# A hybrid encoder layer: SiLU of the next tile's streams and of z moved from the end of a slot to its middle

## Chip, cores and metric

One core of a Trainium2 chip runs the whole kernel. The metric is the device time of one execution in microseconds (us), the median of several runs.

## What is computed

One layer is applied to a prompt of 2048 positions and to a small batch of 8 x 16 positions. The prompt takes nearly all of the time. Cut to what matters here:

```python
p = rms_norm(x, norm1) @ w_in                    # 3080 columns: u_a v_a q k v z beta a
u_a, v_a = gelu(u_a), gelu(v_a)                  # group A: gMLP in blocks of 128 positions
y_a = rms_norm(u_a * (W_s @ v_a + b_s))
q, k, v = silu(causal_conv(q, k, v))             # group B: gated DeltaNet, 4 heads of 128
o, S = delta_rule(l2norm(q), l2norm(k), v, beta, g)   # needs the inverse of a triangular matrix
y_b = rms_norm(o, gdn_norm) * silu(z)
x = x + concat(y_a, y_b) @ w_o
x = x + (silu(h2 @ w_gate) * (h2 @ w_up)) @ w_down    # h2 = rms_norm(x, norm2)
```

## The kernel before

The kernel has two phases, one after the other. The first (`prompt_phase`) computes the token mixing of the prompt, the second (`out_phase`) the feed-forward part. The change touches the first phase alone.

The first phase works on 16 tiles of 128 positions. Two jobs are interleaved by hand on every engine. The background job is the dense work: items of 24 matmuls (three for each of 8 slices of the contraction, because fp32 values are split in a high and a low part), each item cut in four quarters of 6 matmuls. The items are the columns of w_in for 4 tiles at once and, in the last four slots, the product with w_o. The foreground job is the mixing of one tile t. A slot is 25 quarters long and holds the mixing of one tile; slot numbers run from -4 to 15, and `upto(t, n)` issues the background's quarters until n of slot t are out. The order of the instructions of every engine is fixed by this; the engines meet at semaphores only.

The background's steps on ScalarE (ACT) are `split_weights` (L675, the high part of the weights, at a quarter's part 1), `keep_item` (L695, L698 and L701, a copy of a finished item out of PSUM, at part 2) and `split_h` (L687). VectorE (DVE) makes the low parts (L1015, L1021), the taps of the convolution (L1030 to L1047) and, in the last slots, additions (L1077, L1081). TensorE (PE) waits at the start of item n for the low part of its weights, and for item n-2 to have been copied or added, since two PSUM banks take turns. L1535 to L1537 are the three matmuls.

The foreground on ACT, in a slot t: key norms (L891 to L898), values (L905), then six levels of the inverse. In level l PE makes a product (`level_lx`, L1850), ACT copies it (L915), PE makes the next (`level_xlx`, L1864, and L1870 for the last levels), DVE subtracts (L1403) and turns (L1406), and PE's next level starts. Two quarters lie in each level. Behind them come delta (L927), the output (L934), the decays of tile t+1 (L880, L883) and the output's norm (L873, L875). DVE multiplies with the norm (L1455) and with silu(z) (L1459), and TensorE turns v_a of the next tile (L1792). At the end of the slot ACT loads the table of SiLU, takes SiLU of 12 blocks of 128 columns of tile t+1 (k, q and v, `silu_streams`, L859), SiLU of z of tile t (`silu_z`, L863), then the two GELUs of tile t+1 (`gelu_streams`, L866 and L869), and loads the table of Ln and Exp again (L669). The ACT_TABLE_LOAD at L866 is in front of the first GELU: GELU has a table other than SiLU's. DVE needs SiLU of the streams at L1355, PE at L1811 and L1817; `gelu_streams` ends with what PE's transposes into bank gs (L1752 among them) wait for.

Streams and z are stored to DRAM by the background and loaded again by SyncE (SP) with `load_z(t)` (L504) and `load_streams(t + 1)` (L497), both behind quarter 8 of slot t. Where t + 1 is the first of four tiles, `load_streams` comes behind quarter 24 instead, since the background has just made these streams.

Of the kernel before, what the change touches and what calls it, by code (L numbers as in the profile page):

```python
# [70 lines left out]
MACRO = 4  # L71
# [72 lines left out]
def prompt_phase(nc, sh, region, a, a_s):  # L144

    TILES = a["x"].shape[0]
# [33 lines left out]
    with nc.cleanup_on_exit(), ExitStack() as ctx:  # L180
# [166 lines left out]
        def past(eng, semaphore, count):  # L347

            if count > 0:
                eng.wait_ge(semaphore, count)  # L350
# [30 lines left out]
        def fronted(t):  # L381

            return t + 2 * MACRO if t + 2 * MACRO < TILES else None
# [282 lines left out]
        def _(act):  # L666
            def exp_and_ln():

                act.preload_act_table_set("natural_log_exp_and_others")  # L669
# [158 lines left out]
            def front(m, rows, spare=None):  # L828
                if 0 < m < MACRO:
                    act.wait_ge(row_first[m - 1], 16)  # L830
                elif m < TILES:
                    act.wait_ge(s["x_loaded"], 16 * (m - MACRO + 2 if m else 1))
                if MACRO <= m < TILES:
                    act.wait_ge(s["h_turned"], 2 * m)
                past(act, s["h_ready"], m)
                junk_rows = spare if m < MACRO else h[:] if m < TILES else squares
                act.activation(junk_rows, rows[:], ACT.Square, accum_out=ssum[:]).then_inc(s["squared"], 1)
                act.wait_ge(s["squared"], m + 1)
                act.activation(rstd[:], ssum[:], ACT.Ln, bias=sh["eps"][:], scale=1.0 / D_MODEL).then_inc(s["ln_x"], 1)
                act.wait_ge(s["ln_x"], m + 1)  # L840
                act.activation(rstd[:], rstd[:], ACT.Exp, scale=-0.5).then_inc(s["rstd_ready"], 1)

            def gates_raw(j):
                act.wait_ge(s["ba_turned"], j + 1)
                past(act, s["b1_ready"], j)
                act.activation(small[:, 0], gs_cols[:, :, P - 8:P - 4], ACT.Exp, scale=-1.0).then_inc(s["eb_raw"], 1)
                act.wait_ge(s["nax_ready"], j + 1)
                act.activation(small[:, 3], small[:, 2], ACT.Exp).then_inc(s["ex_ready"], 1)
                act.wait_ge(s["ex_ready"], j + 1)
                act.activation(small[:, 4], small[:, 3], ACT.Ln, bias=1.0).then_inc(s["lnx_ready"], 1)  # L850

            def gates_of(j):
                act.wait_ge(s["small_pe"], j + 1)
                past(act, s["s_ready"], MACRO * (j - 1))
                act.activation(gates[:, j % 2], gs_small, ACT.Exp).then_inc(s["gates_ready"], 1)

            def silu_streams(t):
                act.wait_ge(rc_loaded[t % 2], 16 * (t // 2 + 1))
                act.activation(rc[:, t % 2, 0:12], rc[:, t % 2, 0:12], ACT.Silu).then_inc(s["silu_ready"], 1)  # L859

            def silu_z(t):
                act.wait_ge(z_loaded, 16 * (t + 1))
                act.activation(z[:], z[:], ACT.Silu).then_inc(s["z_ready"], 1)  # L863
# [7 lines left out]
            def rsqrt(src, count, ln_sem, ready, t, scale, bias):  # L871
                act.wait_ge(count, t + 1)
                act.activation(r[:], src, ACT.Ln, bias=bias, scale=scale).then_inc(ln_sem, 1)  # L873
                act.wait_ge(ln_sem, t + 1)
                act.activation(r[:], r[:], ACT.Exp, scale=-0.5).then_inc(ready, 1)  # L875
# [9 lines left out]
            def key_norms(t):  # L885
                act.wait_ge(s["k_turned"], t + 1)
                past(act, s["root_k_ready"], t)
                for h_ in range(H_B):
                    if h_ > 0:
                        act.wait_ge(s["ssk_ready"], t * H_B + h_)  # L890
                    act.activation(junk[:], heads[1][:, h_], ACT.Square, accum_out=k_norm[:, 0, h_:h_ + 1])\  # L891
                       .then_inc(s["ssk_ready"], 1)
                act.wait_ge(s["ssk_ready"], (t + 1) * H_B)
                act.activation(k_norm[:, 1], k_norm[:, 0], ACT.Ln, bias=sh["eps"][:]).then_inc(s["ln_k"], 1)
                act.wait_ge(s["ln_k"], t + 1)
                past(act, s["beta_n_ready"], t)
                act.activation(k_norm[:, 2], k_norm[:, 1], ACT.Exp, scale=-1.0).then_inc(s["inv_k_ready"], 1)
                act.activation(k_norm[:, 3], k_norm[:, 1], ACT.Exp, scale=0.5).then_inc(s["root_k_ready"], 1)  # L898

            def scaled_values(t):  # L900
                act.wait_ge(s["v_turned"], t + 1)
                act.wait_ge(s["root_k_ready"], t + 1)
                past(act, s["delta_pe"], t)
                for h_ in range(H_B):
                    last = act.activation(v_rows[:, h_], heads[0][:, h_], ACT.Copy, scale=k_norm[:, 3, h_:h_ + 1])  # L905
                last.then_inc(s["v_rows_ready"], 1)

            def query_squares(t):
                act.wait_ge(s["silu_ready"], t + 1)
                past(act, s["sso_pe"], t)  # L910
                act.activation(sq_q[:], rc[:, t % 2, 4:8], ACT.Square, scale=math.sqrt(EPS * DK * DV)).then_inc(s["sq_q_ready"], 1)

            def level(l, t):
                act.wait_ge(s["lx_pe"], levels(t, l))
                act.activation(halves(LX[l], l, 0), half_bank(gb[0], l), ACT.Copy).then_inc(s["lx_ready"], 1)  # L915

            def gmlp_squares(t):
                act.wait_ge(s["ya_mul"], t + 1)
                past(act, s["ssa_pe"], t)
                act.activation(sq_a[:], ya[:], ACT.Square).then_inc(s["sq_a_ready"], 1)  # L920
                act.activation(sq_a_hi[:], ya[:], ACT.Square).then_inc(s["sq_a_hi_ready"], 1)

            def scale_delta(t):
                act.wait_ge(s["delta_pe"], t + 1)
                past(act, s["s_pe"], t)
                for h_ in range(H_B):
                    last = act.activation(delta[:, h_], heads[1][:, h_], ACT.Copy, scale=beta_n[:, h_:h_ + 1])  # L927
                last.then_inc(s["delta_ready"], 1)
# [11 lines left out]
            def slot(t):  # L940
                j = (t + MACRO) // MACRO
                if t >= 0:
                    upto(t, 4)
                    key_norms(t)
                    upto(t, 5)
                    scaled_values(t)
                    query_squares(t)
                if (t + MACRO) % MACRO == 1 and j < MACROS:
                    upto(t, 8)
                    gates_raw(j)  # L950
                    upto(t, 9)
                    gates_of(j)
                if fronted(t) is not None:
                    upto(t, 9)
                    front(fronted(t), xf)
                if t >= 0:
                    for l in range(LV):
                        upto(t, 10 + 2 * l)
                        level(l, t)
                        upto(t, 11 + 2 * l)  # L960
                        if l == 1:
                            gmlp_squares(t)
                        if l == 3:
                            past(act, s["o_norm_ready"], t)
                            rsqrt(heads[4], s["ssa_pe"], s["ln_a"], s["ra_ready"], t, 1.0 / C_A, sh["eps"][:])
                    upto(t, 22)
                    scale_delta(t)
                    upto(t, 23)
                    output_squares(t)
                if 0 <= t + 1 < TILES:  # L970
                    upto(t, 24)
                    decays(t + 1)
                upto(t, SLOT)
                if t >= 0:
                    output_norm(t)
                    act.preload_act_table_set("silu_and_others")
                if 0 <= t + 1 < TILES:
                    silu_streams(t + 1)
                if t >= 0:
                    silu_z(t)  # L980
                if 0 <= t + 1 < TILES:
                    if t + 1 < DONE:
                        upto(t + 1, 1)
                    gelu_streams(t + 1)
                    exp_and_ln()
# [19 lines left out]
            for t in range(-MACRO, TILES):  # L1005
                slot(t)
# [1618 lines left out]
```

## Time and profile before

| | |
|---|---|
| median of 3 runs | 2964.78 us (2962.66 to 2965.72) |
| the profiled execution | 2964.59 us, of which the span of the instructions is 2962.9 us |
| PE busy | 2822.6 us (95%) |
| DVE busy | 1463.1 us (49%) |
| ACT busy | 976.0 us (33%) |
| mean granted clock of TensorE | 0.979 |
| first phase with its start | 0 to 1326.2 us of the span |

In the rows of a timeline below, the first number is the start and the second the duration; the bracket is how long the engine had been idle and what ended it. Times count from the start of the span. A pair of consecutive instructions on ACT or DVE can overlap by some 0.1 us, so the distance between starts is the better price of a step inside a chain.

### The profile page before, as it was taken

To read this page: it belongs to the slowest core of one execution; us is meant where nothing else is said; L and a number is where in the kernel's file an instruction comes from. 1 tells how busy PE (TensorE), PEld (TensorE's weight loads), DVE (VectorE), ACT (ScalarE), POOL (GpSimd) and SP (SyncE) were. 2 spreads that over 40 slices of the span, in tenths; PEclk is the share of its full clock that TensorE was granted. 3 is DMA by queue.
4 is the path that set the end of the run, shared out by engine and by line. 5 is a ranking of instruction groups with operands and counts; after the bars stand their busy time and mean duration, and the time that the engine had idled before them with its cause. 6 is when DMAs were issued, how large, how long until landed. Compare 5 with 4: busy or idle time off the path is not lost.

```text
span 2962.9 us, 39747 instructions
## 1 busy us (share of the span) xinstructions
PE 2822.6 (95%) x15928; PEld 2553.4 (86%) x15928; DVE 1463.1 (49%) x2055; ACT 976.0 (33%) x1619; POOL 171.3 (6%) x155
## 2 busy tenths in 40 slices
PE   7999899899989898869999999999999999999998
PEld 6877787788878777769999999899999999999998
DVE  3666666567656645653434343533333345343344
ACT  3335445544544544432111111421212133222222
POOL 1001111111111111100000000000000000000000
PEclk9899999999999999989999999999999999999999
DMA  8255333343433384645121212522121243222220
GB/s 289 81 162 163 104 118 114 114 131 94 153 107 101 118 152 146 206 139 160 57 71 57 71 57 71 185 60 68 57 70 57 73 139 97 75 71 71 85 71 36
DMA packets 361875, 314.72 MB, mean 106 GB/s; under 512 B 15653, under 2 KB 315762, under 8 KB 359714
## 3 DMA queue, kind: packets, MB, share of 16 engines
q1 hardware_dynamic: 361762, 313.20, 35.4%
q8 instruction: 72, 1.18, 0.2%
q14 instruction: 41, 0.34, 0.0%
HBM read 254.80 MB, written 58.36 MB: 106 GB/s over the span
## 4 chain that ended last, share of the span: by engine, by line
PE 53%; DVE 1%; ACT 1%; issue 0%; DMA 0%; POOL 0%; DVEq 0%; ACTq 0%; POOLq 0%
PE gate_ps L2459 6%; PE gate_ps L2461 6%; PE gate_ps L2460 6%; PE up_ps L2460 6%; PE up_ps L2459 6%; PE up_ps L2461 6%; PE down_ps L2460 5%; PE down_ps L2459 5%; PE down_ps L2461 5%; DVE w_in_sb L2453 0%; ACT h_hi L2252 0%; DVE w_in_sb L2353 0%; DVE h_lo L2375 0%; ACT w_hi L2233 0%; DVE w_in_sb L2397 0%
## 5 line engine op out<-in xcount | busy, mean ns | idle before, releaser
L1535 PE MATMUL pr_p<-hT_hi_p,w_hi_p 128*128 128x512 f32 x992 | 432.7, 436 | 44.3 <-ACT w_in_sb L701 21.5
L1537 PE MATMUL pr_p<-hT_hi_p,w_lo_p 128*128 128x512 f32 x992 | 397.6, 401 | 0.0
L1536 PE MATMUL pr_p<-hT_lo_p,w_hi_p 128*128 128x512 f32 x992 | 395.2, 398 | 0.0
L2459 PE MATMUL gate_ps<-h_hi,w_hi 128*128 128x384 f32 (+1 forms) x1056 | 346.2, 328 | 18.1 <-DVE h_lo L2375 15.4
L2339 DVE TENSOR_TENSOR w_in_sb<-up_ps,w_in_sb 128x384 f32<-128x384 f32 (+1 forms) x132 | 70.7, 535 | 589.7 <-PE up_ps L2461 589.7
L2461 PE MATMUL gate_ps<-h_hi,w_lo 128*128 128x384 f32 (+1 forms) x1056 | 345.9, 328 | 0.0
L2460 PE MATMUL gate_ps<-h_lo,w_hi 128*128 128x384 f32 (+1 forms) x1056 | 345.7, 327 | 0.0
L2459 PE MATMUL up_ps<-h_hi,w_hi 128*128 128x384 f32 (+1 forms) x1056 | 344.0, 326 | 0.0
L2460 PE MATMUL up_ps<-h_lo,w_hi 128*128 128x384 f32 (+1 forms) x1056 | 343.9, 326 | 0.0
L2461 PE MATMUL up_ps<-h_hi,w_lo 128*128 128x384 f32 (+1 forms) x1056 | 343.9, 326 | 0.0
L2353 DVE TENSOR_TENSOR w_in_sb<-down_ps,w_in_sb 128x1024 f32<-128x1024 f32 x187 | 228.7, 1223 | 182.7 <-PE down_ps L2461 181.8
L2459 PE MATMUL down_ps<-wd_hi,act_hi 128*128 128x512 f32 x748 | 291.7, 390 | 2.3 <-DVE w_in_sb L2353 2.3
L2460 PE MATMUL down_ps<-wd_lo,act_hi 128*128 128x512 f32 x748 | 291.5, 390 | 0.0
L2461 PE MATMUL down_ps<-wd_hi,act_lo 128*128 128x512 f32 x748 | 291.5, 390 | 0.0
L1535 PEld LDWEIGHTS pr_p<-hT_hi_p,w_hi_p 128*128 128x128 f32 x992 | 192.4, 194 | 85.1 <-issue 41.8
L2244 ACT ACTIVATE act_hi<-w_in_sb 128x384 fp32r<-128x384 f32 (+1 forms) x132 | 67.1, 508 | 527.1 <-DVE w_in_sb L2339 527.1
L1015 DVE TENSOR_TENSOR w_lo_p<-w_in_sb,w_hi_p 128x1024 fp32r<-128x1024 f32 x124 | 157.0, 1266 | 149.5 <-ACT w_hi_p L675 149.0
L1537 PEld LDWEIGHTS pr_p<-hT_hi_p,w_lo_p 128*128 128x128 f32 x992 | 190.9, 192 | 44.5
L1536 PEld LDWEIGHTS pr_p<-hT_lo_p,w_hi_p 128*128 128x128 f32 x992 | 192.9, 194 | 35.1 <-issue 5.0
L2459 PEld LDWEIGHTS gate_ps<-h_hi,w_hi 128*128 128x128 f32 x1056 | 199.9, 189 | 20.2 <-issue 19.0
L661 POOL TENSOR_TENSOR w_in_sb<-mt_p,link 128x512 f32<-128x512 f32 x96 | 149.5, 1564 | 942.7 <-DVE mt_p L1369 666.2
L2460 PEld LDWEIGHTS gate_ps<-h_lo,w_hi 128*128 128x128 f32 x1056 | 199.8, 189 | 1.2
(359 smaller groups left out, 4610.9 us busy)
## 6 DMA issues: line engine op xcount, KB each, us to landing
w_in_sb<-in_w_in SPq DMA_DIRECT2D x100, 512.0 KB, 4.3
w_in_sb<-in_w_gate SPq DMA_DIRECT2D x66, 512.0 KB, 4.0
w_in_sb<-in_w_up SPq DMA_DIRECT2D x66, 512.0 KB, 5.2
w_in_sb<-in_w_down SPq DMA_DIRECT2D x33, 1024.0 KB, 4.8
stream_tiles<-w_in_sb SPq DMA_DIRECT2D x96, 256.0 KB, 2.5
w_in_sb<-stream_tiles SPq DMA_DIRECT2D x16, 1280.0 KB, 7.3
w_in_sb<-mixed_tiles SPq DMA_DIRECT2D x29, 512.0 KB, 4.4
out<-w_in_sb SPq DMA_DIRECT2D x21, 512.0 KB, 3.5
```

The costliest lines, as they stand in the source:

```text
L661: pool.tensor_tensor(lt[:, l % 2], mt[:], over_heads(sh["link"][:, l + 1, :]), ALU.mult)\
L1015: dve.tensor_tensor(w_lo[:, n % RING_W], wraw[:, n % 2], w_hi[:, n % RING_W].bitcast(F32), ALU.subtract)\
L1535: pe.matmul(out, w_h, x_h, start=start, stop=False)
L1536: pe.matmul(out, w_h, x_l, start=False, stop=False)
L1537: return pe.matmul(out, w_l, x_h, start=False, stop=stop)
L2244: act_e.activation(act_hi[:, c, h * half:(h + 1) * half], act[:, h, 0:half], ACT.Copy)\
L2339: dve.tensor_tensor(act[:, h, 0:half], up_ps[h][:, 0:half], gate_act[:, h, 0:half], ALU.mult)\
L2353: dve.tensor_tensor(acc[:, t, :], down_ps[t % 2][:].rearrange("p a b -> p (a b)"), acc[:, t, :], ALU.add).then_inc(added[t], 1)
L2459: pe.matmul(out, w_h, x_h, start=start, stop=False)
L2460: pe.matmul(out, w_h, x_l, start=False, stop=False)
L2461: return pe.matmul(out, w_l, x_h, start=False, stop=stop)
```

## The change

In slots whose next tile is not the first of four, SiLU of the next tile's streams is taken behind the step of level l = 2 (the third level) instead of at the slot's end. SiLU of z is taken there in all slots. In front of them the table of SiLU is loaded, behind them that of Ln and Exp. At the end of the slot the load of SiLU's table is no longer asked for; `silu_streams` stays there for the first tile of each four (t = -1, 3, 7, 11).

```diff
+            def early_streams(t):
+                return t < TILES and t % MACRO > 0
+
             def silu_z(t):
                 act.wait_ge(z_loaded, 16 * (t + 1))
                 act.activation(z[:], z[:], ACT.Silu).then_inc(s["z_ready"], 1)
@@
                         upto(t, 11 + 2 * l)
                         if l == 1:
                             gmlp_squares(t)
+                        if l == 2:
+                            act.preload_act_table_set("silu_and_others")
+                            if early_streams(t + 1):
+                                silu_streams(t + 1)
+                            silu_z(t)
+                            exp_and_ln()
                         if l == 3:
                             past(act, s["o_norm_ready"], t)
                             rsqrt(heads[4], s["ssa_pe"], s["ln_a"], s["ra_ready"], t, 1.0 / C_A, sh["eps"][:])
@@
                 upto(t, SLOT)
                 if t >= 0:
                     output_norm(t)
-                    act.preload_act_table_set("silu_and_others")
-                if 0 <= t + 1 < TILES:
+                if 0 <= t + 1 < TILES and not early_streams(t + 1):
                     silu_streams(t + 1)
-                if t >= 0:
-                    silu_z(t)
                 if 0 <= t + 1 < TILES:
                     if t + 1 < DONE:
                         upto(t + 1, 1)
```

## Rows read from the trace of the kernel before

**Rows 1.** Busy time in one stretch, the second phase: length, busy PE, PEld, DVE, ACT, POOL, granted clock, DMA.

```profile
1326.20:2962.90 1636.70, 1621.03 (x9101) 1529.09 (x9101) 657.40 (x620) 378.65 (x479) 0.00 (x0) 1.00 0.26 81
```

**Rows 2.** The waits of PE: releaser, us in total, times, longest us.

```profile
PE pr_p L1535 <- ACT w_in_sb L701: 21.5, 9, 4.3
```

**Rows 3.** Timeline of ACT, end of slot 8.

```profile
834.73 1.28 ACT L976 ACT_TABLE_LOAD   x1
836.02 1.49 ACT L859 ACTIVATE w_in_sb<-w_in_sb 128x1536 f32<-128x1536 f32 x1
837.42 0.61 ACT L863 ACTIVATE z_p<-z_p 128x512 f32<-128x512 f32 x1
837.93 1.05 ACT L675 ACTIVATE w_hi_p<-w_in_sb 128x1024 fp32r<-128x1024 f32 x1
839.00 1.28 ACT L866 ACT_TABLE_LOAD   x1
...
842.72 0.60 ACT L701 ACTIVATE w_in_sb<-pr_p 128x512 f32<-128x512 f32 x1
```

**Rows 4.** Timeline of PE behind the ends of slots 8 and 9.

```profile
843.46 0.77 PE L1535 MATMUL pr_p<-hT_hi_p,w_hi_p 128*128 128x512 f32 x1 [4.27 <-ACT w_in_sb L701]
...
846.16 1.05 PE L1811 MATMUL gb_p<-ident,w_in_sb 128*128 128x128 f32 x4
...
909.01 0.47 PE L1535 MATMUL pr_p<-hT_hi_p,w_hi_p 128*128 128x512 f32 x1 [0.82 <-ACT w_in_sb L701]
...
911.86 0.60 PE L1811 MATMUL gb_p<-ident,w_in_sb 128*128 128x128 f32 x4
```

**Rows 5.** PE in one stretch: length, busy, granted clock, DMA share, GB/s.

```profile
843.40:848.00 4.60, 4.54 (x15) 0.50 0.81 218
```

**Rows 6.** Timeline of ACT, levels 2 and 3 of slot 2.

```profile
419.03 0.39 ACT L915 ACTIVATE w_in_sb<-gb_p 128x256 f32<-128x256 f32 x1 [2.98 <-PE gb_p L1850]
420.51 1.06 ACT L675 ACTIVATE w_hi_p<-w_in_sb 128x1024 fp32r<-128x1024 f32 x1 [1.09 <-PE pr_p L1537]
424.02 0.39 ACT L915 ACTIVATE w_in_sb<-gb_p 128x256 f32<-128x256 f32 x1 [2.45 <-PE gb_p L1850]
```

**Rows 7.** Timeline of PE, the products behind these copies in slot 2.

```profile
425.26 1.00 PE L1864 MATMUL gb_p<-w_in_sb,XT_p 128*128 128x64 f32 x8
...
427.94 0.44 PE L1850 MATMUL gb_p<-X_p,w_in_sb 128*128 128x64 f32 x3
```

**Rows 8.** Timeline of DVE, the same stretch of slot 2.

```profile
422.95 1.18 DVE L1015 TENSOR_TENSOR w_lo_p<-w_in_sb,w_hi_p 128x1024 fp32r<-128x1024 f32 x1
424.06 2.43 DVE L1047 SCALAR_TENSOR_TENSOR w_in_sb<-w_in_sb,cols 128x512 f32<-128x512 f32 x2
426.41 0.41 DVE L1403 TENSOR_TENSOR X_p<-X_p,gb_p 128x256 f32<-128x256 f32 x1
```

**Rows 9.** Timelines of DVE and of PE at the start of slot 3.

```profile
452.62 0.69 DVE L1459 TENSOR_TENSOR w_in_sb<-ya_p,z_p 128x512 f32<-128x512 f32 x1 [2.63 <-ACT z_p L863]
...
457.35 1.23 DVE L1015 TENSOR_TENSOR w_lo_p<-w_in_sb,w_hi_p 128x1024 fp32r<-128x1024 f32 x1 [2.48 <-ACT w_hi_p L675]
...
466.40 1.08 PE L1850 MATMUL gb_p<-X_p,w_in_sb 128*128 128x64 f32 x8 [1.80 <-issue]
471.85 0.88 PE L1864 MATMUL gb_p<-w_in_sb,XT_p 128*128 128x64 f32 x6 [2.06 <-DVE w_in_sb L1391]
```

**Rows 10.** Timeline of PE, behind the ends of slots 12, 13 and 14.

```profile
1100.88 0.77 PE L1535 MATMUL pr_p<-hT_hi_p,w_hi_p 128*128 128x512 f32 x1 [5.63 <-DVE w_in_sb L1077]
...
1167.66 0.47 PE L1535 MATMUL pr_p<-hT_hi_p,w_hi_p 128*128 128x512 f32 x1 [1.75 <-DVE w_in_sb L1077]
...
1238.80 0.45 PE L1752 MATMUL gs_p<-ident,w_in_sb 128*128 128x128 f32 x1 [3.62 <-issue]
```

**Rows 11.** SP's issue of the streams' load in slot 12, and the landing of L497's loads in all slots.

```profile
1048.45 0.32 SPq L497 DMA_DIRECT2D w_in_sb<-stream_tiles  x1
...
DMA to landing us min/median/max: 6.2/7.3/11.3
```

## The prediction

> **What bounds the kernel now.** I read the busy time by stretches first. The second phase is 1636.70 us with PE busy for 1621.03 of them [rows 1]; the change doesn't touch it, so what it can win lies in the first 1326 us. There the waits of PE came next. One group leads straight to ScalarE: item starts that wait for the copy L701, 21.5 us in 9 waits [rows 2]. Then I read the timelines of all engines around the end of each slot. PE is full between the stalls, so each us of such a stall that goes is a us of the span, as long as the next wait of PE doesn't take it back.
>
> The end of slot 8 shows how a long stall arises. ACT finishes the output's norm at 834.73. Then come a table load, SiLU of the streams, SiLU of z, a weight split, the load of GELU's table, two GELUs and the load of Ln and Exp, and only then the copy L701, at 842.72 [rows 3]. PE starts again at 843.46 after 4.27 us [rows 4]. Its clock is then granted at 0.50, the 1.2 GHz level, until 848.00 [rows 5]: the quarter behind it takes 846.16 - 843.46 = 2.70 us. The same 4.27 us stall stands behind slots 0, 4 and 8.
>
> **What the change does to the slot's end.** Where the streams go early (12 of the 16 slots with a next tile), the end loses L976, L859 and L863. In distances between starts that is 837.93 - 834.73 = 3.20 us with the weight split behind it, or 3.3 with a table load behind it, as a load starts only when the activation before has ended [rows 3]. The load of GELU's table stays, since it is in the code of L866 and not asked for by the removed line. In slots 3, 7 and 11 the streams stay, and SiLU's table must still be loaded, now in front of L859: only z goes, 0.51 us. In slot 15 table and z go: about 1.26 us, from DVE's side.
>
> *Slots 0, 4, 8.* The stall falls from 4.27 to about 1.07, so 3.2 us each. With 1.07 us I expect no fall of the clock: the stall of 0.82 at 909.01 is followed by a matmul of 0.47 us, that of 4.27 by one of 0.77 [rows 4]. The quarter behind takes about 1.4 us (two quarters lie between 909.01 and 911.86) in place of 2.70, and ACT's key norms follow PE's L1811, whose last transpose also comes 0.4 sooner. Together 4.9 each. Of these I take back 1.35, an estimate, in slots 0 and 8, whose slow stretch is the longest: the chain through DVE behind it doesn't follow fully, and PE meets it after a longer wait. Sum: 3 x 4.9 - 2 x 1.35 = 12.0.
>
> *Slots 1, 5, 9.* The 0.82 us stall of L701 goes [rows 4], in two of them with a wait of 0.3 us for DVE later: 3.0.
>
> *Slots 2, 6, 10.* No stall is at the end itself, but DVE waits 2.63 us for z and again 2.48 for the weight split, and it runs late into the next slot: PE waits 1.80 at 466.40 and 2.06 at 471.85 for it [rows 9]. With z ready and the split 3.33 us sooner, DVE's chain starts 3.33 us sooner. PE's two waits are 3.86 us, so DVE stays the bound and the gain is 3.33 each: 10.0.
>
> *Slots 3, 7, 11.* 0.5 each: 1.6.
>
> *Slots 12 to 15.* Behind slot 12 PE waits 5.63 us for an addition on DVE that is queued behind L1015, which is behind ACT's block [rows 10]; it comes 3.33 sooner, and 1.5 of the slow clock goes: 4.8. Behind slot 13 a stall of 1.75 goes, for an addition queued on DVE behind z. Behind slot 14 PE waits 3.62 for the end of `gelu_streams` [rows 10]: 3.3 goes, and some of the slow clock, 3.8. Slot 15's last chain starts 1.26 sooner. Sum: 11.6.
>
> Gain at the ends: 12.0 + 3.0 + 10.0 + 1.6 + 11.6 = 38.2 us.
>
> **What it costs in the middle.** The new block is two loads of 1.28 and the two SiLUs, 1.39 and 0.61 in their chain: 4.63 us with the gaps [rows 3], or 3.2 where only z moves. It stands between the copies L915 of levels 2 and 3, which are 424.02 - 419.03 = 4.99 us apart [rows 6], and ACT is nearly idle there. Behind the copy of 0.39 it ends at 5.02. So what counts is what else ACT has to do there.
> - Slots 1, 5, 9, 12, 13: nothing. Level 3's copy is on time.
> - Slots 0, 4, 8: L695, a copy as long as L701, 0.60 [rows 3]. The copy is 0.5 late. In slot 2 its product on PE starts at 425.26, 0.85 behind the copy's end [rows 6, 7], and the others have the same: hidden.
> - Slots 3, 7, 11: only z, behind a split and a copy: on time within 0.1.
> - Slots 2, 6, 10, 14: the split L675, which ran at 420.51, is now queued behind the block and in front of the copy. The copy is 0.96 late, against 0.85 less about 0.1 for the semaphore: 0.2 us of stall. And DVE's L1015 waits for this split: it started at 422.95 and can now start at about 425.1. Behind it are two taps and then L1403, which started at 426.41, and PE's next product at 427.94 [rows 7, 8]. With the taps at 0.75 each, L1403 would come at 427.7; with the 2.43 us that the pair took before, at 428.6. PE starts some 0.55 behind L1403, so it waits 0.3 to 1.2. I take 0.8, nearer to the middle as the pair was slowed by something else then running, and the same for all four: 3.2 us.
>
> The two SiLUs now need their data in mid-slot. SP issues the streams of slot 12 at 1048.45; level 2's copy there ends 13 us later, and no load took more than 11.3 us [rows 11]. That is the closest slot. No transfer moves in SP's queue, and z's buffer is read by DVE at the slot's end as before. ACT has 16 loads more in all, some 20 us of 976, which costs nothing while the block lies in the 5 us gap; if the gap is gone, each us is a us of PE.
>
> The sum is 38.2 - 3.2 = 35.0 us. From the profiled execution's own 2964.59 us, 0.2 below the median, this gives 2929.6, said as 2930.
>
> The Trainium skill ("ScalarE: Activation LUTs", What ACT_TABLE_LOAD costs) says that a switch of tables costs a load of about 1283 ns and a drain of about 1380 ns more. This trace agrees with the load, 1.28, but not with the drain: L859 starts 0.01 us behind the load's end, and L976 0.02 behind the activation before [rows 3]. By the page's figure, an estimate, the block would be 7.4 us long.
>
> **The rivals.**
> *Given back (part).* The stalls at the slots' ends shrink, but PE meets the same DVE chain and loses there what it won; the slow stretches of the clock stay. Then count the direct shortening alone: 3 x 3.2 + 3 x 0.8 + 1.6 + 3.3 + 1.75 + 3.3 + 1.3 = 23, half of the 10 of slots 2, 6, 10, less 5 in the middle, and another 5 for the relocated waits: 18 us, 2947. For it: DVE waits stand in many slots. Against it: DVE itself waits for ACT in exactly these places [rows 9].
> *No change.* The block in mid-slot delays the chain as much as the end wins, or other waits of PE grow. 2965. It needs 2.2 us of delay in each of 16 slots, and the arithmetic above finds it in none.
> *Slower.* One mechanism: level 3's copy L915 stands in ACT's queue behind the block, and everything of the inverse behind the copy. If the block is longer than it looks, because a table load between activations in this place needs more than 1.28 or SiLU waits for a stream that lands late, each us above about 0.7 comes 16 times. It decides from 2.9 us extra (a block of 7.5) on; at 3.5 us extra the time would be 2964.6 - 38 + 16 x 2.8, 2971. The Trainium skill's drain, in the section named above, would bring such an amount if it were paid here. Against it: all loads in the trace are 1.28 and the streams land in time.
> *Not as described.* The compiler places a table load of its own anywhere in the new order. Each adds 1.28 in a place with or without slack; this is inside the range.
>
> **How the numbers follow.** Forecast (2918 to 2940): 0.60. Given back in part (2940 to 2958): 0.24. No change within 0.2%, 6 us, which is about what a measurement of this kernel can tell: 0.07. Slower: 0.09. The lower end, 2918, is the forecast with more of the slow clock won back (1.7 us for each of some eight stalls); the upper end, 2956, takes in the gain without the DVE chains and the full 1.2 us in mid-slot. Faster 0.84, same 0.07, slower 0.09.
>
> **What would show it.** The ACT timeline should have L866's load right behind L875 at a slot's end, and in mid-slot a load, L859, L863 and a load between two L915. L701 as releaser of PE should fall from 21.5 us to about 8.5. DVE's wait for z at L1459 should be gone. PE's waits at L1850 and L1864 of slots 3, 7, 11 should be about 0 and 0.5. L1850 or L1864 should show new waits below 1.2 us in slots 2, 6, 10, 14 only. Waits of PE for L915 in all slots would speak for the slower rival; unchanged sums of waits at L1781 plus L1850 plus L1752 that grow by what L701 lost, for the second. The prediction is wrong if the block in mid-slot is longer than 5 us.

## The result: 38 us faster

| | before | after |
|---|---|---|
| median | 2963.72 us (2961.26 to 2965.72) | 2925.42 us (2924.59 to 2930.75) |
| the profiled execution | 2964.59 us, span 2962.9 | 2924.59 us, span 2922.9 |
| PE busy | 2822.6 us | 2812.6 us |
| ACT busy | 976.0 us | 1001.6 us |
| second phase | 1636.70 us [rows 1] | 1636.70 us |
| first phase with its start | 1326.2 us | 1286.2 us |

The ratio is 0.9875, with a 95% interval from 0.9858 to 0.9892: 38.3 us between the medians, and 40.0 between the two profiled executions. The predicted time was 2930. The second phase takes the same 1636.70 us, so all of the gain lies in the first phase. The lines of the changed code are some 3 to 6 higher in the profile of after: L915 is L918, L866 is L869, L1015 is L1021, L1403 is L1409, L1850 is L1856, L1864 is L1870.

The waits of PE after (releaser, us in total, times, longest us) answer to [rows 2]:

```profile
PE gs_p L1758 <- DVE w_in_sb L1310: 14.4, 7, 3.8
...
PE pr_p L1541 <- ACT w_in_sb L701: 9.2, 6, 2.2
...
PE gb_p L1856 <- DVE X_p L1409: 6.7, 8, 2.1
```

The copy L701 held PE up for 21.5 us before, the largest sum of all, and holds it up for 9.2 now. DVE leads the waits instead.

ACT's timeline at the end of slot 8, the place of [rows 3]:

```profile
814.85 1.04 ACT L675 ACTIVATE w_hi_p<-w_in_sb 128x1024 fp32r<-128x1024 f32 x1
815.91 1.28 ACT L869 ACT_TABLE_LOAD   x1
817.20 0.63 ACT L869 ACTIVATE w_in_sb<-w_in_sb 128x512 f32<-128x512 f32 x1
...
819.63 0.60 ACT L701 ACTIVATE w_in_sb<-pr_p 128x512 f32<-128x512 f32 x1
```

From the weight split to the copy it is 4.78 us, as before (842.72 - 837.93 = 4.79). What stood in front of the split, one load and two SiLUs, is gone and nothing stands in its place. PE's timeline behind it, the place of [rows 4]:

```profile
820.38 0.47 PE L1541 MATMUL pr_p<-hT_hi_p,w_hi_p 128*128 128x512 f32 x1 [0.95 <-ACT w_in_sb L701]
...
821.83 0.60 PE L1817 MATMUL gb_p<-ident,w_in_sb 128*128 128x128 f32 x4
```

The stall is 0.95 us instead of 4.27, the first matmul takes 0.47 instead of 0.77, and the quarter behind it 1.45 instead of 2.70. The clock of PE in the first 4.60 us behind it (length, busy PE, PEld, DVE, ACT, POOL, granted clock, DMA share, GB/s) is the full 2.4 GHz, where [rows 5] show 0.50:

```profile
820.30:824.90 4.60, 4.52 (x28) 3.94 (x29) 0.00 (x0) 2.27 (x12) 0.00 (x0) 1.00 0.80 217
```

In the middle of a slot ACT now does this; slot 2, the place of [rows 6]:

```profile
412.27 0.38 ACT L918 ACTIVATE w_in_sb<-gb_p 128x256 f32<-128x256 f32 x1 [2.98 <-PE gb_p L1856]
412.67 1.28 ACT L967 ACT_TABLE_LOAD   x1
413.96 1.49 ACT L859 ACTIVATE w_in_sb<-w_in_sb 128x1536 f32<-128x1536 f32 x1
415.36 0.61 ACT L866 ACTIVATE z_p<-z_p 128x512 f32<-128x512 f32 x1
415.99 1.28 ACT L669 ACT_TABLE_LOAD   x1
417.28 1.06 ACT L675 ACTIVATE w_hi_p<-w_in_sb 128x1024 fp32r<-128x1024 f32 x1
418.25 0.36 ACT L918 ACTIVATE w_in_sb<-gb_p 128x256 f32<-128x256 f32 x1
```

The block is 417.28 - 412.67 = 4.61 us long. Level 3's copy comes 5.98 us behind level 2's, not 4.99 as in [rows 6], since the split stands between them. It is 0.99 us late.

**Where the gain lies.** The distance between the ends of the output's norm (L875, L878 after) of two neighbouring slots says what each slot's end and the slot behind it won.

| slots' ends | won, us | sum | forecast |
|---|---|---|---|
| 0, 4, 8 | 4.35, 4.88, 3.74 | 13.0 | 12.0 |
| 1, 5, 9 with the middle of 2, 6, 10 | 0.57, 0.63, 0.13 | 1.3 | 3.0 - 2.4 |
| 2, 6, 10 | 4.32, 2.74, 4.24 | 11.3 | 10.0 |
| 3, 7, 11 | 0.52, 0.52, 0.10 | 1.1 | 1.6 |
| 12, 13, 14 | 5.70, 1.17, 3.63 | 10.5 | 10.35 - 0.8 |
| 15 | 1.5 | 1.5 | 1.25 |

That makes 38.7. Another 1.3 us lies ahead of the end of slot 0, where the block in slot 0's middle is all that changed, and that can win nothing: I take it for the scatter of one execution. Another execution of the changed kernel, the control below, bears this out: slot 0 ends there at 318.94 us, against 318.95 before and 317.71 in the execution of the table. It also shows how far the table can be trusted: the rows agree within 0.4 us, but for slots 2, 6 and 10, which won 1.1, 2.8 and 4.2 us, 8.1 in sum and not 11.3. PE's waits of more than 0.25 us from 75 us on fell from 109.7 to 78.7 us in sum, 31.0 less. The stretches at the half clock that begin between 200 us and the start of the second phase are 92.2 us in sum before and 71.7 after, 20.5 less, which is 10 us of work. Together they are 41, beside the 40.0 by which the spans differ.

### The profile page after: what moved, and what is told of

Read it like the earlier page. It is cut to its first block, busy times and chain, and to the rows that moved or that the text cites. A ratio compares the mean times of both kernels' runs of the same rounds, so it can differ in the third digit from the quotient of the medians.

```text
span 2922.9 us, 39766 instructions
## 1 busy us (share of the span) xinstructions
PE 2812.6 (96%) x15928; PEld 2548.1 (87%) x15928; DVE 1460.3 (50%) x2055; ACT 1001.6 (34%) x1638; POOL 168.6 (6%) x155
## 4 chain that ended last, share of the span: by engine, by line
PE 54%; DVE 1%; ACT 1%; issue 0%; DMA 0%; DVEq 0%; POOL 0%; ACTq 0%; POOLq 0%
PE gate_ps L2465 6%; PE gate_ps L2467 6%; PE gate_ps L2466 6%; PE up_ps L2465 6%; PE up_ps L2466 6%; PE up_ps L2467 6%; PE down_ps L2466 5%; PE down_ps L2465 5%; PE down_ps L2467 5%; DVE w_in_sb L2459 0%; DVE h_lo L2381 0%; ACT h_hi L2258 0%; DVE w_in_sb L2359 0%; ACT w_hi L2239 0%; DMA w_in_sb<-h_tiles 0%
## 5 line engine op out<-in xcount | busy, mean ns | idle before, releaser
L1021 DVE TENSOR_TENSOR w_lo_p<-w_in_sb,w_hi_p 128x1024 fp32r<-128x1024 f32 x124 | 161.3, 1301 | 146.2 <-ACT w_hi_p L675 145.8
L2467 PEld LDWEIGHTS gate_ps<-h_hi,w_lo 128*128 128x128 f32 x1056 | 199.7, 189 | 0.0
```

The lines of the kernel that those rows point to most:

```text
L1021: dve.tensor_tensor(w_lo[:, n % RING_W], wraw[:, n % 2], w_hi[:, n % RING_W].bitcast(F32), ALU.subtract)\
L2467: return pe.matmul(out, w_l, x_h, start=False, stop=stop)
```

## The experiments

Twelve runs follow: ten further kernels, one of them twice, and the changed kernel once more. All times are medians; "faster by" is against the kernel before on the same chip, which had 2964.73 us beside the first four, 2963.65 beside the next four and 2965.44 beside the last four. All of them do the same computation; two load tables that nothing needs. Diffs are against the changed kernel.

**The two SiLUs, one at a time.** Only z in the middle:

```diff
-                return t < TILES and t % MACRO > 0
+                return False
```

> Only SiLU of z goes to mid-slot (with its two table loads); SiLU of the streams stays at the end in all slots, with its own load. My theory, that what counts is the time of ACT's chain at the slot's end: it gets only 0.5 us shorter, so some 0.5 us in each of 13 slots, 1.75 more behind slot 13 and 0.8 more at the very end, where DVE waits for z itself: 9 us below the kernel before, 2955. Rival, that DVE's own wait for z (40.7 us in 16 waits) is what kept the next slot late: 20 us or more below. DVE's wait for z is gone in both.

Only the streams in the middle, with z and the load of SiLU's table in front of it at the end of the slot again:

```diff
-                        if l == 2:
+                        if l == 2 and early_streams(t + 1):
                             act.preload_act_table_set("silu_and_others")
-                            if early_streams(t + 1):
-                                silu_streams(t + 1)
-                            silu_z(t)
+                            silu_streams(t + 1)
...
                     output_norm(t)
+                    act.preload_act_table_set("silu_and_others")
...
+                if t >= 0:
+                    silu_z(t)
```

> Only SiLU of the streams goes to mid-slot; z and the load of SiLU's table stay at the end. My theory: the chain at the end is 1.4 us shorter, the slow clock behind slots 0, 4 and 8 stays: 3 x 1.4 + 3 x 0.8 + 3 x 1.4 + 1.4 + 1.4 = 14 us, less 1 in mid-slot: 13 us below before, 2951. Together with z alone that is 22, well short of 38, and the rest belongs to the table load that goes only when both go. Rival, that the two parts add up to the whole: 25 to 30 us below.

The first ran in 2955.48 us (ratio 0.9973, 0.9964 to 0.9983), 9.3 us faster than before; the second in 2954.51 (0.9967, 0.9954 to 0.9979), 10.2 faster. Both came near what was expected, and neither rival holds. Each alone leaves L701 with 18.5 and 14.9 us of waits. The sum is 19.5, half of the 38.3 that both give. What is left, 18.8 us, belongs to neither.

**The load alone.** The changed kernel, with the load of SiLU's table asked for at the end of every slot as before, where nothing uses it:

```diff
                     output_norm(t)
+                    act.preload_act_table_set("silu_and_others")
```

> The changed kernel with the load of SiLU's table left at the slot's end, where nothing uses it. My theory: 1.3 us come back wherever the end bounds the next slot (slots 0, 2, 4, 6, 8, 10, 12, 14 and 15, and part of 1, 5, 9) and some of the slow clock behind slots 0, 4 and 8: 12 to 16 us above the changed kernel. Rival, that shortening the end beyond z and the streams was given back at the next wait for DVE: no more than 3 us above.

2941.07 us (0.9919, 0.9902 to 0.9935), 23.7 faster than before: the load costs 38.3 - 23.7 = 14.6 us, as expected. At the ends of slots 3, 7 and 11 the changed kernel has it too, since the streams stay there. So this kernel has 13 loads more (1651 instructions on ACT against 1638), 16.7 us, and some 1.1 us of each reached the end. The waits of PE of this kernel show both ways in which it does:

```profile
PE pr_p L1542 <- ACT w_in_sb L701: 13.4, 6, 2.4
...
PE gb_p L1871 <- DVE w_in_sb L1398: 6.2, 3, 2.1
```

L701 has 4.2 us more in the same 6 places, and a wait for DVE's L1398 is among the large ones again (L1391 in [rows 9], L1397 in the changed kernel). So the load accounts for most of the 18.8 us that neither half gave: it stands there for whichever SiLU stays, and the load at the slot's end goes only when the last SiLU has left it.

**Only some slots.** The change in slots 0, 4 and 8 alone, the others as before:

```diff
-                return t < TILES and t % MACRO > 0
+                return t in (1, 5, 9)
...
-                        if l == 2:
+                        if l == 2 and t % MACRO == 0 and t < 12:
...
+                    if t not in (0, 4, 8):
+                        act.preload_act_table_set("silu_and_others")
...
+                if t >= 0 and t not in (0, 4, 8):
+                    silu_z(t)
```

> The change in slots 0, 4 and 8 alone; all others as before. My theory: each gains 4.0 to 4.9 us, of which 3.3 is the stall of PE for L701 and the rest the clock behind it: 12.5 us below before, 2951. Rival, given back at the wait for L1331 in mid-slot: 5 us below.

And in slots 2, 6 and 10 alone, by the same edit with (3, 7, 11) and (2, 6, 10):

> The change in slots 2, 6 and 10 alone; all others as before. No stall of PE stands at the end of these slots, so all of the gain must come through DVE's chain into the next one. My theory, now with the trace of the changed kernel: DVE makes the first X 3.3 us sooner, PE's waits in slots 3, 7, 11 fall from 4.3 to about 2, with the slow clock 3 to 4 us each, less 0.6 to 1 in mid-slot: 8 to 10 us below before, 2955. Rival, that only shortened stalls at L701 matter: no more than 2 us below.

The first ran in 2952.84 us (0.9963, 0.9951 to 0.9976), 10.8 faster; its three slots won 4.2, 4.5 and 3.4 us, 12.1 in sum. The second ran in 2955.63 (0.9965, 0.9953 to 0.9977), 9.8 faster. Neither rival holds. In the second, L701 keeps PE waiting for 21.5 us in 9 waits, just as before: no stall at a slot's end went, and the gain came through DVE's chain and the clock behind it. In its profiled execution slots 3, 7 and 11 are 1.14, 4.31 and 2.66 us shorter, 8.1 in sum, and the block in the middle of slots 2, 6 and 10 costs 0.62, 0.57 and 0.97 us, 2.2 in sum.

**A longer block.** The decision point of the prediction's slower rival was a block 2.9 us longer. Two loads more, which nothing needs, make it 2.57 us longer, 7.18 us in all, somewhat short of that point:

```diff
                             exp_and_ln()
+                            act.preload_act_table_set("silu_and_others")
+                            exp_and_ln()
```

> The changed kernel with two more table loads, 2.57 us, behind the block in mid-slot. My theory: the gap between the copies of levels 2 and 3 is full, so level 3's copy is 2.6 us late in every slot and PE waits 1.8 to 2.8 for it, less what is paid already: some 30 us above the changed kernel, and PE's waits for L915's counterpart appear in all 16 slots. Rival, that there is slack behind in the chain of levels: 10 us above or less.

2972.62 us (1.0026, 1.0016 to 1.0035): 7.9 us slower than before, 46 above the changed kernel. A new wait leads the list of PE's waits, for level 3's copy, in 15 slots; PE's timeline has one of them in slot 2:

```profile
PE gb_p L1872 <- ACT w_in_sb L918: 29.2, 15, 2.6
```

```profile
428.07 1.10 PE L1872 MATMUL gb_p<-w_in_sb,XT_p 128*128 128x64 f32 x8 [2.58 <-ACT w_in_sb L918]
```

The direct waits are as expected; 17 us came on top. The time at the half clock is 92.2 us again, as before the change (some 10 us of work), and DVE waits longer for ACT's weight split, 171.0 us in place of 145.8. So the gap between the two copies is full: a block of 4.61 us cost little there, and one of 7.18 us costs more than the whole gain.

**The block two levels later, in slots 2, 6, 10 and 14.** There the split stands in the way at level 2.

```diff
-                        if l == 2:
+                        if l == (4 if t % MACRO == 2 else 2):
```

> The changed kernel with the block behind level 4 in slots 2, 6, 10 and 14, where the levels are 5.4 us apart and the weight split behind it is not needed at once. My theory: the 0.6 to 1.0 us that level 3 and 4 are late there go: 3 us below the changed kernel, 2922. Rival, that the same wait arises one level on: equal.

2925.00 us (0.9868, 0.9851 to 0.9884), 38.7 faster than before and so not to be told from the changed kernel. The four slots won 0.6, 0.6, 1.0 and 0.9 us, 3.0 in sum, as expected. But slot 3 took 62.4 us instead of 60.8, and slot 13 67.3 instead of 66.3. In slot 3 no wait grew by more than 0.04 us, but the clock fell behind one; more on this below. In slot 13 a wait for the addition L1083 grew from 2.31 to 3.29 us, and it did so again in each later run with this edit. Why it grew is open.

**What is left at the slot's end.** The copy L701 still stands behind two GELUs and two loads. It can be taken in front of them:

```diff
                     if t + 1 < DONE:
-                        upto(t + 1, 1)
+                        upto(t + 1, 3)
```

> The changed kernel with three quarters of the background (split and copy L701) in front of the two GELUs at the slot's end in place of one. My theory: the copy no longer stands behind a load, two GELUs and a load, so the waits of PE for L701 (0.95 three times, 2.08 twice) go, and DVE gets its weight split 3.7 us sooner in slots 2, 6 and 10: 8 to 11 us below the changed kernel, 2916. Rival, that the late GELU or ACT's wait for the split's buffer hold something else up: equal or slower.

2922.46 us (0.9865, 0.9849 to 0.9881), 41.2 faster than before, 3 better than the changed kernel where 8 to 11 were expected. L701 is gone from the list of waits. In its place:

```profile
PE gb_p L1856 <- DVE X_p L1409: 12.5, 9, 2.3
```

Against 6.7 us in 8 waits after the change, 5.8 us more went here, where L701 had 9.2. PE meets DVE's chain instead. All of PE's waits of more than 0.25 us are only 1.4 us less in sum than after the change (77.3, against 78.7). So for this further step the rival of a gain that is given back holds, for the most part.

**Both edits**, then the same again beside the changed kernel itself, as a control:

> Block behind level 4 in slots 2, 6, 10, 14, and split and copy in front of the GELUs. If the two are independent: 11 to 14 us below the changed kernel, 2913. If both only feed the same wait for DVE: no better than the better of the two.

> The changed kernel itself, beside the next ones on the same chip, as the measure for small differences: 2925 by any theory.

> Block behind level 4 in slots 2, 6, 10, 14, and split and copy in front of the GELUs, beside the changed kernel on the same chip. If its lead of 5 us is real: 2920. If what it wins at L701 goes to the clock and to waits for DVE in the next slot: within 2 us of the changed kernel.

Both together ran in 2920.41 us (0.9853, 0.9837 to 0.9870), and again in 2922.50 (0.9859, 0.9844 to 0.9875). The changed kernel beside the latter ran in 2928.96 (0.9879, 0.9864 to 0.9894), 36.5 faster than before where it had been 38.3. So one edit's 3 us is at the limit of what such a comparison can tell. Both together win 4.9 us in the first comparison and 6.5 in the second: the lead is real, but it is half of the 11 to 14 of two independent edits.

**The copy first also behind slots 11 and 12**, on top of both edits. There an addition (L1083) of the background stood behind the same ACT block.

```diff
-                    if t + 1 < DONE:
-                        upto(t + 1, 3)
+                    if t + 1 <= DONE + 1:
+                        upto(t + 1, 3 if t + 1 <= DONE else 1)
```

> As the kernel with both edits, and split and copy go in front of the GELUs at the ends of slots 11 and 12 too. My theory: PE's waits of 3.46 behind slot 11 (for L1021's counterpart) and 2.30 behind slot 12 (for L1077's) go, with some slow clock: 6 to 9 us below the kernel with both edits, 2913. Rival, that the next wait takes it: no more than 2 us.

2917.06 us (0.9840, 0.9826 to 0.9853): 48.4 faster than before, 11.9 below the changed kernel beside it and the best that ran. Of PE's waits there:

```profile
PE gb_p L1856 <- DVE X_p L1409: 12.1, 8, 2.3
...
PE pr_p L1541 <- DVE w_in_sb L1083: 7.2, 2, 3.9
PE pr_p L1541 <- DVE hT_lo_p L1027: 6.6, 2, 6.3
```

Against the kernel with both edits this is 2922.50 - 2917.06 = 5.4 us, a little under the 6 to 9 expected and above the rival's 2. The two waits that were named went, 3.46 us for L1027 and 2.32 for L1083. But in slot 12 the next wait for L1083 rose from 1.31 to 3.93 us, so the sum for L1083 is 7.2 us where both edits had 6.9: part of the gain was given back.

## Why the prediction was right

**The ends of slots 0, 4 and 8: right.** The stall went from 4.27 to 0.95 us (forecast 1.07), and the clock no longer fell right behind it: 13.0 us where 12.0 were forecast, and 12.1 where these slots were changed alone. The slow clock did not go altogether. Each of slots 1, 5 and 9 had 10.2 us at the half clock and has 6.8 now, all behind PE's next long wait, for DVE's L1331 (L1337 after), which the change leaves where it was:

```profile
PE gs_p L1781 <- DVE g_p L1331: 11.2, 3, 4.1
```

```profile
PE gs_p L1787 <- DVE g_p L1337: 12.2, 3, 4.1
```

In slot 9 that is this stretch (PE alone before the clock):

```profile
836.10:842.10 6.00, 6.00 (x24) 0.50 0.16 45
```

This wait grew by 0.57 us in slot 1 and 0.44 in slot 9 and not in slot 5. The 1.35 us that the prediction took back in slots 0 and 8 has its sign and its place from this, but they won only 0.5 and 1.1 us less than slot 4.

**Slots 2, 6 and 10: the size near, in part by luck; one step in the path wrong.** DVE's wait for z is gone, and it and PE behind it run so at the start of slot 3, the place of [rows 9]:

```profile
443.86 0.69 DVE L1465 TENSOR_TENSOR w_in_sb<-ya_p,z_p 128x512 f32<-128x512 f32 x1
...
447.88 1.23 DVE L1021 TENSOR_TENSOR w_lo_p<-w_in_sb,w_hi_p 128x1024 fp32r<-128x1024 f32 x1 [1.76 <-ACT w_hi_p L675]
```

```profile
461.47 1.00 PE L1870 MATMUL gb_p<-w_in_sb,XT_p 128*128 128x64 f32 x8
...
466.86 1.08 PE L1856 MATMUL gb_p<-X_p,w_in_sb 128*128 128x64 f32 x8 [2.05 <-DVE X_p L1409]
```

X, with which DVE opens the chain of the inverse (L1385, L1379 before), was ready 13.06 us behind the end of slot 2's norm instead of 16.36, 3.30 sooner, with 3.33 forecast. PE's waits of 1.80 at the first and 2.06 at the second product of a level went; but one of 2.05 appeared at the next product, L1856 (L1850 before), where the prediction had about 0. The two named waits were 3.86 us, and the prediction left 0.5 of them. In slot 3 the three waits of before (1.80, 2.06 and 0.47, 4.33 in all) became this one, which is 2.28 less, and in slots 7 and 11 it is 2.28 and 2.21 less: 6.8 in sum where 10.0 were forecast. The slots still won 11.3, since the clock was added: of the time at the half clock, 3.4 us in each of slots 3, 7 and 11 before, slots 3 and 11 had none left and slot 7 still all of it. At half speed 3.4 us are 1.7 us of work, about the difference between the 4.3 and 4.2 us that slots 3 and 11 won and the 2.7 of slot 7. That share is luck: in the control slot 3 had 6.8 us at the half clock, and the three won 8.1, as they did where they were changed alone. What sets the wait that remains is DVE itself: from L1021 at 447.88 to L1409 at 466.30 it waits for nothing. So "DVE stays the bound" was right, and the credit in the sum was that of the shift alone; that the clock comes on top, and the rest of DVE's queue against it, was not in it.

**Slots 12 to 15: the sizes right.** The addition behind slot 12 and the transposes behind slot 14, the places of [rows 10], on PE:

```profile
1069.58 0.47 PE L1541 MATMUL pr_p<-hT_hi_p,w_hi_p 128*128 128x512 f32 x1 [2.30 <-DVE w_in_sb L1083]
...
1200.64 0.63 PE L1758 MATMUL gs_p<-ident,w_in_sb 128*128 128x128 f32 x4 [0.32 <-issue]
```

5.63 became 2.30, 3.33 less, and 3.62 became 0.32. Both are the length of what left the end of the slot, 3.3 us. Behind slot 14 the forecast of 3.8 was met by other parts than its own: PE ran into waits for DVE's L1310, so all waits of slot 15 are only 1.1 us less (8.3 to 7.2), and the time at the half clock there fell from 10.2 to 3.4 us. Together 3.63 us were won.

**The middle of slots 2, 6, 10 and 14: the sign and the size right, in a place that PE hardly shows.** DVE's timeline, the place of [rows 8]:

```profile
418.38 1.40 DVE L1021 TENSOR_TENSOR w_lo_p<-w_in_sb,w_hi_p 128x1024 fp32r<-128x1024 f32 x1 [2.11 <-ACT w_hi_p L675]
419.70 1.52 DVE L1053 SCALAR_TENSOR_TENSOR w_in_sb<-w_in_sb,cols 128x512 f32<-128x512 f32 x2
421.15 0.41 DVE L1409 TENSOR_TENSOR X_p<-X_p,gb_p 128x256 f32<-128x256 f32 x1
```

L1021 started 6.11 us behind level 2's copy (forecast 425.1 - 419.03 = 6.07). The two taps took 1.52, the lower of the prediction's bounds, not 2.43. L1409 came 8.88 us behind the copy, 1.50 later than the 7.38 of [rows 6, 8]. Level 4's copy came 10.55 us behind level 2's in slot 2 instead of 9.95, and 10.52 instead of 9.55 in slot 10: 0.6 and 1.0, around the 0.8 taken. Of new waits of PE only one of 0.46, in slot 10, is above 0.25; the rest of the delay was in PE's own queue. The block moved to level 4 gave these four slots 3.0 us back, which is the 3.2 of the sum.

**The rival of a gain given back falls.** It had PE meeting the same DVE chain. PE's waits sank by 31.0 us in sum, and in slot 3 three waits became one. The sign named for it was that the waits at L1781, L1850 and L1752 grow by what L701 lost, 12.3 us. Their listed waits for DVE grew from 30.0 to 33.3 us; with those at the same lines that the profile gives no releaser for, they fell from 39.0 to 33.6. DVE itself had waited for ACT in these places, as the prediction argued. What the rival describes did occur for the next step, when L701 was taken first.

**The slower rival falls at its condition, not its mechanism.** With 2.57 us more in the block the kernel is slower by 7.9 us, against 2.9 as the decision point. The mechanism costs even more than the prediction had: 16 times what is above 0.7 us would be 30 us, and it was 46. Without them, the block is 4.61 us long. The Trainium skill ("ScalarE: Activation LUTs", What ACT_TABLE_LOAD costs) adds a drain of about 1380 ns to each switch. The block has two switches in it, and its activations start 0.01 us behind the loads' ends and the loads 0.02 behind the activations; the trace has no room for a drain here, and by this measurement it is not paid. The load itself is the page's 1283 ns:

```profile
L669 ACT ACT_TABLE_LOAD x34 | 43.6, 1283 | 0.6
L869 ACT ACT_TABLE_LOAD x16 | 20.5, 1283 | 0.3
L967 ACT ACT_TABLE_LOAD x16 | 20.5, 1283 | 0.3
L859 ACT ACT_TABLE_LOAD x4 | 5.1, 1283 | 0.1
```

These are the groups of ACT's loads (line, times | busy us, mean ns | idle us before them). L859 has 4 where it had 1: the load that the removed line no longer asks for is placed by itself in front of L859 in slots 3, 7 and 11, as forecast. The prediction's count of 16 loads more forgot these three: ACT has 19 loads more (1638 instructions against 1619), 24 us of the 25.6 by which its busy time grew.

The prediction names two upper ends of its range, 2940 and 2956; the measured 2925.42 lies below both.

## What to carry to other kernels

Moving work from a crowded place on an engine to an idle one is worth what stood behind it there, and not the length of the work: here 38 us, with 19 loads more than before. What shares a table load must move together, or the load stays; halves measured apart show half of the gain. Before moving, measure the gap against the whole of the block with its loads, and look what else of the engine's queue lands in that gap: here 4.6 us of work fitted in 5.0 and cost 3 us in all, and 2.6 us more in the same gap cost 46 more.

## What the runs showed of the hardware

The clock of TensorE didn't fall behind the same wait each time. Behind slot 3's wait of 2.05 us the profiled execution of the changed kernel ran on at the full level. The same program in the control met the same wait, 2.06 us, and the 8 matmuls of 64 columns behind it took 1.94 us instead of 1.08:

```profile
468.20 1.94 PE L1856 MATMUL gb_p<-X_p,w_in_sb 128*128 128x64 f32 x8 [2.06 <-DVE X_p L1409]
```

The two windows of 3.5 us behind the wait (columns as above; the second row has PE alone before the clock):

```profile
466.80:470.30 3.50, 3.44 (x25) 3.21 (x26) 3.47 (x4) 1.54 (x3) 1.83 (x1) 1.00 0.05 15
```

```profile
468.20:471.70 3.50, 3.50 (x12) 0.50 0.02 6
```

The granted clock is 1.00, the 2.4 GHz level, in the first, with 25 matmuls in it; it is 0.50, the 1.2 GHz level, in the second, with 12. In the control the half clock lasted 6.8 us, and slot 3 took 63.99 us instead of 60.77. The kernel with the block at level 4 met 2.09 us there and fell too, and its slot 3 was 1.6 us longer. A few waits of about 2 us in a kernel whose time is otherwise the same within 0.1% are thus worth up to 3 us each, up or down, which is as much as one of the smaller edits here. What decides it is left open: no run here varied it.

A tap on DVE (L1053, 128x512) takes 0.74 us, but 1.78 at 468.68, while POOL's tensor operation L661 runs from 468.08 for 1.83 us, instead of the 1.30 that it takes at 417.40. The same pair in slot 2 had 2.43 us before [rows 8], and the change moved it out of POOL's way: 1.52. Each of the two is slow where they overlap in these rows; a shift by 1 us decides whether they do.
